# Two prompt tiles served head by head: an interleaved job order and a shorter lead-in

## The chip, the core and the metric

The kernel runs on one NeuronCore of a Trainium2 chip. The metric is the device time of one execution in microseconds. The engines are TensorE (PE), VectorE (DVE), ScalarE (ACT), GpSimd (POOL, which here issues the gathers) and SyncE (SP, which issues plain loads). Each executes its own instructions in program order and waits on semaphores. All loads run on the core's 16 DMA engines.

## What is computed

One step of a hybrid decoder layer for a prompt of 512 tokens and a sample group of 32, in float32. The trunk (S5 scan, convolution module, cross-attention, three gates and `w_out`) gives `h`; then comes the part that takes most of the time, a layer of 16384 single-neuron experts:

```python
q = (xb @ w_q).reshape(tb, 8, 2, 128)                 # 8 heads, two halves
s = einsum('thpc,pkc->thpk', q, sub_keys)             # 128 scores for each half
sv, si = top_k(s, 16)
cand = sv[:, :, 0, :, None] + sv[:, :, 1, None, :]    # 16 x 16 sums
cv, ci = top_k(cand.reshape(tb, 8, 256), 16)          # 16 experts per token and head
gate = softmax(cv)
act = gelu(einsum('thkd,td->thk', u_tab[experts], xb))
out = einsum('thk,thkd->td', gate * act, v_tab[experts])
```

and at last `y = rmsnorm(h + out)`.

## The kernel before

**Tiles and jobs.** Tokens lie in tiles of 128: t = 0 to 3 for the prompt, t = 4 for the samples, which share two jobs. A job is a pair (t, h) of tile and head; there are 34 in the list `EXPERTS`, and each gathers 16 times: gather g = 16·n + j fetches, for job n and choice j, one row of u and v (8 KB together) for each of 128 tokens, 1.05 MB in all.

**Trunk first for the first 256 tokens.** The trunk runs for tokens 0 to 255 (tiles 0 and 1) before the experts begin. Head 0's queries are made beside the last products of `w_out`. `first_query`/`first_queries` make the queries of one head for both tiles (jobs `Aq{h}.{b}` on the PSUM banks, 8 matmuls each), `first_scores` the scores (`As{h}.{b}`, two matmuls each), again for both tiles at once. ACT copies them to the score buffers `sc(n)`, one per job. `EARLY_HEADS` heads have queries and scores made ahead of the expert loop (with the query of one more head).

**The late list.** Everything else on PE, in `rest_of_trunk`, is threaded through the loop: the other heads of tiles 0 and 1, then for tokens 256 to 543 the gates and projections (`g{q}.{b}` with 8 matmuls, `p{q}.{b}` with 4), `w_out` (`w0` to `w7`), 15 empty steps, the sum of squares (`ssb`), transposes (`ht`, `xt`), queries `q{h}.{b}` (8 each) and scores `s{h}.{b}` (3 each). One step of this list, a matmul or an empty step, is called a unit here. After each gather j PE does 2 units, or 6 where j % 4 is 3 (`late_matmuls`). `PLACE[name]` is the gather in whose units a job ends. DVE and ACT do their part of a late job at a fixed number of gathers behind PLACE: DVE multiplies and adds a gate product at PLACE + 8 (L1926, L1931), adds a `w` job at PLACE + 8 (L1937), and ACT copies `ht` jobs at PLACE + 2 (L1344). Before `w0` PE waits until the last merge is done (`pe.wait_ge(mergeb_ok, 2 * KD)`). DVE reads `ssb` at PLACE + 8 (L1940) and two gathers later makes the 8 blocks of `xbT_b` (L1943 to L1949).

**The loop on each engine.**
- DVE: for each gather a dot product with u (`dot`, L1876); every fourth, behind j % 4 = 0, `weigh` (L1891) makes the weights of the four gathers before; for the jobs 0 to 11 the choices 3, 7, 11, 15 are added by DVE itself (`add_row`, L1902, behind the dot with j % 4 = 1); behind j = 10 `add_rest` (L1915) adds PE's sum of the job before to `h2(t)`. Between the dots it executes pieces of `route(n + 2)`, the two top-16 searches that give job n + 2 its experts. `route(0)` and `route(1)` run ahead of the loop.
- ACT: per four gathers a gelu (L1274), per PE gather a scaled identity matrix (`diag`, L1407), once a job the exponentials of the softmax (`exp_of`, L1267).
- PE: for each gather not added by DVE, two matmuls of 512 columns with the scaled identity (L1058), and then the units.
- POOL issues gather g into a ring of `RING = 10` rows when row g − 10 has been used: `pool.wait_ge(v_used[by], count)`.
- SP loads weight tiles of 512 KB (projections 256 KB) into four places, the m-th when the product of the (m − 4)-th is done.

In the trace one float32 matmul counts as two entries.

## Time and profile before

| | us |
|---|---|
| median of 3 runs | 1969.55 (1967.14 to 1969.92) |
| the profiled execution | 1968.79 |
| its span on the core | 1967.2 |
| first gather issued at | 469.35 |
| busy in the span: PE / DVE / POOL / ACT | 1697.1 / 1367.2 / 661.6 / 526.7 |
| moved by the DMA engines | 674.10 MB, of which gathers (software queue) 577.23 MB |
| first entries of the chain that ended last, by engine | PE 47%, DMA 36%, issue 8% |

Times in the rows are in us from the start of the span. In the order of time a row gives its start, its length, engine, line, operation, output and input, how many entries it joins, and in brackets how long the engine was idle before and who released it. In a table of stretches a row gives the stretch, its length, the busy time of PE, PEld, DVE, ACT and POOL with the number of instructions, then the granted clock of PE (1.00 is the level of 2.4 GHz, 0.50 that of 1.2), the busy share of the DMA engines and what they moved in GB/s.

### The profile page before, as it was taken

The page shows a single profiled execution, that of the slowest core. Times are in us where ns is not written, and L with a number is a line of the kernel's source. Part 1 is how long each engine was busy: PE and PEld are TensorE (multiplying, and loading weights), DVE is VectorE, ACT ScalarE, POOL GpSimd, SP SyncE. Part 2 cuts the span into 40 slices and gives each one's busy share as a digit, 9 for nine tenths or more (in the row PEclk, how much of TensorE's full clock was granted, in tenths as well). Part 3 has the DMA queues.
Part 4 walks back from the last instruction along what each step waited for, and adds up shares of the span by engine and source line. Part 5 has one row for each costly group of instructions (what it writes and reads, how often), then busy time and mean ns, then how long its engine had stood idle before and what let it go on. Part 6 is the DMA issues. An engine that isn't in the chain of part 4 may idle for free.

```text
span 1967.2 us, 17805 instructions
## 1 busy us (share of the span) xinstructions
PE 1697.1 (86%) x5491; PEld 1011.1 (51%) x5491; DVE 1367.2 (69%) x3363; ACT 526.7 (27%) x1211; POOL 661.6 (34%) x605
## 2 busy tenths in 40 slices
PE   8999999999899999978989987778777767767876
PEld 7888887888555555544455543333333212323332
DVE  5998573334777777767977667777777777777755
ACT  3121143202243433312333322222222212222221
POOL 1020030001344444433443444434434444444442
PEclk9989999999999999989899999988989999998899
DMA  5452453555999999989999999999999999999996
GB/s 208 138 86 97 159 126 118 154 181 206 419 419 418 418 417 416 416 329 420 385 422 419 407 389 421 421 421 417 413 417 415 421 421 417 414 422 396 414 421 286
DMA packets 112111, 674.10 MB, mean 343 GB/s; under 512 B 12720, under 2 KB 15104, under 8 KB 42000
## 3 DMA queue, kind: packets, MB, share of 16 engines
q0 software_dynamic: 80816, 577.23, 72.2%
q1 hardware_dynamic: 30640, 94.82, 14.0%
q10 hardware_dynamic: 560, 0.92, 0.2%
q8 instruction: 44, 0.72, 0.1%
q14 instruction: 51, 0.42, 0.1%
HBM read 665.79 MB, written 6.21 MB: 342 GB/s over the span
## 4 chain that ended last, share of the span: by engine, by line
PE 47%; DMA 36%; issue 8%; DVE 4%; ACT 2%; POOL 2%; ACTq 0%; POOLq 0%; DVEq 0%; SPq 0%
DMA upper<-in_peer_uv,upper 22%; PE pair L1058 19%; DMA lower<-in_peer_uv,upper 13%; PE pair L616 7%; PE pair L627 6%; PE pair L979 5%; PE pair L929 2%; PE pair L810 1%; ACT upper L1407 1%; DVE upper L1876 1%; POOL upper L592 1%; POOL lower L592 1%; PE pair L661 1%; PE pair L671 1%; PE pair L798 1%
## 5 line engine op out<-in xcount | busy, mean ns | idle before, releaser
L1058 PE MATMUL pair<-upper 128*128 128x512 f32 (+1 forms) x1184 | 582.7, 635 | 135.8 <-ACT upper L1407 135.8
L592 POOL DMA_INDIRECT upper<-in_peer_uv,upper x324 | 372.8, 1151 | 493.4 <-PE pair L1058 429.6
L1058 PE MATMUL pair<-lower,upper 128*128 128x512 f32 (+1 forms) x792 | 383.9, 627 | 92.8 <-ACT upper L1407 92.8
L1058 PEld LDWEIGHTS pair<-upper 128*128 128x128 f32 (+1 forms) x1184 | 225.9, 197 | 430.0 <-issue 281.6
L592 POOL DMA_INDIRECT lower<-in_peer_uv,upper x220 | 249.3, 1133 | 498.7 <-PE pair L1058 316.0
L1058 PEld LDWEIGHTS pair<-lower,upper 128*128 128x128 f32 (+1 forms) x792 | 149.8, 195 | 286.9 <-issue 188.5
L1876 DVE CUSTOM_DVE_ANT_0 upper<-upper 128x1024 f32<-128x1024 f32 x172 | 210.7, 1225 | 121.5 <-DMA upper<-in_peer_uv,upper 121.5
L1876 DVE CUSTOM_DVE_ANT_0 upper<-upper,lower 128x1024 f32<-128x1024 f32 x152 | 186.0, 1224 | 97.4 <-DMA upper<-in_peer_uv,upper 97.2
L1407 ACT ACTIVATE upper<-upper 128x128 f32<-128x128 f32 (+1 forms) x494 | 164.7, 386 | 296.2 <-DVE upper L1891 296.0
L1876 DVE CUSTOM_DVE_ANT_0 lower<-lower,upper 128x1024 f32<-128x1024 f32 x116 | 142.1, 1225 | 87.8 <-DMA lower<-in_peer_uv,upper 87.7
L1274 ACT ACTIVATE upper<-upper 128x4 f32<-128x4 f32 x136 | 33.7, 248 | 627.3 <-DVE upper L1876 627.2
L979 PE MATMUL pair<-lower 128*128 128x288 f32 x704 | 185.1, 407 | 0.0
L1876 DVE CUSTOM_DVE_ANT_0 lower<-lower 128x1024 f32<-128x1024 f32 x104 | 127.2, 1223 | 71.1 <-DMA lower<-in_peer_uv,upper 71.0
L979 PEld LDWEIGHTS pair<-lower 128*128 128x128 f32 x704 | 133.7, 191 | 65.9 <-issue 37.7
L616 PE MATMUL pair<-lower 128*128 128x272 f32 x576 | 133.1, 393 | 1.5 <-ACT lower L1138 1.5
L616 PEld LDWEIGHTS pair<-lower 128*128 128x128 f32 x576 | 109.3, 190 | 24.5 <-issue 2.2
L979 PE MATMUL pair<-upper,lower 128*128 128x288 f32 x256 | 72.2, 416 | 10.7 <-DVE upper L1931 10.7
L1603 DVE SCALAR_TENSOR_TENSOR upper<-upper 128x512 f32<-128x512 f32 x120 | 80.5, 745 | 0.0
L627 PE MATMUL pair<-lower 128*128 128x256 f32 x336 | 75.4, 379 | 0.0
L979 PEld LDWEIGHTS pair<-upper,lower 128*128 128x128 f32 x256 | 49.9, 196 | 43.2 <-issue 22.5
L1274 ACT ACT_TABLE_LOAD x56 | 71.8, 1283 | 1.0
L627 PEld LDWEIGHTS pair<-lower 128*128 128x128 f32 x336 | 63.3, 190 | 8.4
(364 smaller groups left out, 1736.3 us busy)
## 6 DMA issues: line engine op xcount, KB each, us to landing
lower<-in_w_in SPq DMA_DIRECT2D x64, 512.0 KB, 7.2
lower<-in_peer_q SPq DMA_DIRECT2D x32, 512.0 KB, 8.0
lower<-in_proj SPq DMA_DIRECT2D x48, 256.0 KB, 7.0
lower<-in_w_out SPq DMA_DIRECT2D x16, 512.0 KB, 4.6
upper<-in_peer_uv,upper POOLq DMA_INDIRECT x324, 11.7
upper<-in_cache_k SPq DMA_DIRECT2D x8, 512.0 KB, 4.5
upper<-in_cache_v SPq DMA_DIRECT2D x8, 512.0 KB, 3.7
lower<-in_peer_uv,upper POOLq DMA_INDIRECT x220, 11.7
```

The costliest lines, as they stand in the source:

```text
L592: pool.indirect_dma_start(row(g), None, a["peer_uv"], bass.IndirectOffsetOnAxis(ap=idx[:, n % 8, j:j + 1], axis=0)).then_inc(row_in[g % RI ...
L616: mm = pe.matmul(ps[:, h, 0:HT], w[:, j, :], rhs[:, j, h * HT:(h + 1) * HT], start=(j == 0), stop=(j == k - 1))
L627: mm = pe.matmul(one_bank(ps), w[:, j, :], rhs[:, j, 0:FIRST], start=(j == 0), stop=(j == k - 1))
L661: mm = pe.matmul(ps[:, 0, 0:MEM], w[:, k, :], memT[:, k, :], start=(k == 0), stop=(k == KD - 1))
L671: mm = pe.matmul(ps[:, m, (j - 1) * P:(j + 1) * P], memT[:, k, m * P:(m + 1) * P], wring[:, s0:s0 + 2, k * P:(k + 1) * P], start=(k == 0), ...
L929: mm = pe.matmul(ps[:, 0:FIRST], w[:, k, :], xbT[:, k, :], start=(k == 0), stop=(k == KD - 1))
L979: mm = pe.matmul(ps[:, 0:REST], w[:, j, :], x[:, j, :], start=(j == 0), stop=(j == k - 1))
L1058: mm = pe.matmul(pairs[n % 2][0:rows, h, :], diag[:, (nth - 1) % DIAGS, 0:rows], row(g)[:, D + h * 512:D + (h + 1) * 512], start=(j == min ...
L1274: act.activation(gel[:, n % 2, j:j + GROUP], dots[:, n % 2, j:j + GROUP], ACT.Gelu, scale=rcol[:, t:t + 1] if t < 2 else 1.0).then_inc(gel ...
L1407: act.activation(diag[:, nth % DIAGS, 0:cols], turn, ACT.Copy, scale=weight[:, n % 8, j:j + 1]).then_inc(diag_ok, 1)
L1603: stt(v, tail, w, v, ALU.mult, ALU.add).then_inc(conv_step, 1)
L1876: dve.tensor_tensor_reduce(u, u, xb(EXPERTS[n][0]), 1.0, 0.0, ALU.mult, ALU.add, dots[:, n % 2, j:j + 1]).then_inc(u_used, 1)
```

## The change

Three edits. The list of jobs: the sixteen jobs of the tiles 0 and 1 alternate between the tiles, (0,0), (1,0), (0,1), (1,1) and so on, where they were (0,0) to (0,7) and then (1,0) to (1,7); the jobs from 16 on stay. `EARLY_HEADS` goes from 4 to 2. And ACT writes the scores of head h to the buffers 2h and 2h + 1, with the two exponentials `exp_of(0)` and `exp_of(1)` both behind the scores of head 1.

```diff
-EARLY_HEADS = 4
+EARLY_HEADS = 2
...
-EXPERTS = ([(t, h) for t in range(3) for h in range(PH)] + [(4, 0), (4, 1)] + [(3, h) for h in range(PH)])
+EXPERTS = ([(t, h) for h in range(PH) for t in range(2)] + [(2, h) for h in range(PH)] + [(4, 0), (4, 1)] + [(3, h) for h in range(PH)])
...
-                    act.activation(sc(h)[:, b, :], ps[:, 0:P], ACT.Copy, scale=rcol[:, 0:1])
-                    act.activation(sc(8 + h)[:, b, :], ps[:, P:2 * P], ACT.Copy, scale=rcol[:, 1:2]
+                    act.activation(sc(2 * h)[:, b, :], ps[:, 0:P], ACT.Copy, scale=rcol[:, 0:1])
+                    act.activation(sc(2 * h + 1)[:, b, :], ps[:, P:2 * P], ACT.Copy, scale=rcol[:, 1:2]
...
-                if h != 2:
-                    exp_of(h // 2)
+            for n in range(LAG):
+                exp_of(n)
```

`BANK_JOBS` and `PLACE` are worked out from `EARLY_HEADS`. The jobs Aq3, As2, Aq4 and As3 enter the late list with 16, 4, 16 and 4 units. PLACE moves so:

| job | before | after |
|---|---|---|
| As2.1 | ahead of the loop | 7 |
| As7.1 | 21 | 35 |
| p7.2 | 117 | 131 |
| w0 | 119 | 133 |
| ssb | 147 | 159 |
| q7.1 | 217 | 231 |
| s7.1 | 226 | 239 |

On PE, ahead of the loop and at its first gather (L929 are queries, L944 scores, L1058 the gather's product), one piece of the difference:

```order
 L929 MATMUL pair<-upper,lower 128x256 x32
 L944 MATMUL pair<-upper,lower 128x128 x4
-L929 MATMUL pair<-upper,lower 128x256 x16
-L944 MATMUL pair<-upper,lower 128x128 x4
-L929 MATMUL pair<-upper,lower 128x256 x16
-L944 MATMUL pair<-upper,lower 128x128 x4
 L1058 MATMUL pair<-lower,upper 128x512 x2
```

The queries of heads 3 and 4 and the scores of heads 2 and 3 are no longer there.

On PE, at the entry to w0 (the L979 that waits for `mergeb_ok`), before: behind gather 118, with 8 matmuls up to gather 120.

```order
L1058 MATMUL pair1<-upper 128x512 [waits diag_ok]
L1058 MATMUL pair1<-upper 128x512
L979 MATMUL pair3<-upper,lower 128x288 [waits bank_free2,late_w_in0,mergeb_ok]
L979 MATMUL pair3<-upper,lower 128x288 x7
L1058 MATMUL pair1<-lower,upper 128x512 [waits diag_ok]
```

After: behind gather 130 and the last four matmuls of p7.2, with 4 matmuls up to gather 132.

```order
L1058 MATMUL pair0<-lower,upper 128x512
L979 MATMUL pair2<-upper,lower 128x288 [waits bank_free1,late_w_in3]
L979 MATMUL pair2<-upper,lower 128x288 x3
L979 MATMUL pair3<-upper,lower 128x288 [waits bank_free2,late_w_in0,mergeb_ok]
L979 MATMUL pair3<-upper,lower 128x288 x3
L1058 MATMUL pair0<-lower,upper 128x512 [waits diag_ok]
```

The place moved by 12 gathers on PE, and w0 is cut in other pieces (4, 2 and 2 matmuls where 8 stood in a row).

On DVE, at that last merge (L1931), before: behind the dot of gather 125, which is one behind a weighing.

```order
L1876 ISA upper<-upper,lower 128x1024 [waits row_in5]
L1876 ISA upper 128x1
L1902 SCALAR_TENSOR_TENSOR upper<-lower,upper 128x1024 [waits acc_step,w_ok]
L1926 TENSOR_TENSOR lower<-lower,pair2 128x288 [waits acc_step,bank_full1,bank_free0]
L1931 TENSOR_TENSOR upper<-upper,lower 128x288 [waits bank_free1,mergeb_ok]
```

After: behind the dot of gather 139, with L1915 just ahead of that dot.

```order
L1915 TENSOR_TENSOR upper<-upper,pair1 128x1024 [waits v_used_by_pe,acc_step]
L1876 ISA upper<-upper,lower 128x1024 [waits row_in9]
L1876 ISA upper 128x1
L1860 TENSOR_TENSOR upper<-upper 128x256 [waits dve_step]
L1863 TENSOR_REDUCE upper<-upper 128x16 [waits dve_step]
L1926 TENSOR_TENSOR lower<-lower,pair2 128x288 [waits bank_full1,bank_free0]
L1931 TENSOR_TENSOR upper<-upper,lower 128x288 [waits bank_free1,mergeb_ok]
```

The merge moved by 14 gathers on DVE, w0's first matmul by 12 on PE.

## Rows read from the trace of the kernel before

**Rows 1.** The page, the DMA rate in 40 equal slices of the span

```profile
GB/s 208 138 86 97 159 126 118 154 181 206 419 419 418 418 417 416 416 329 420 385 422 419 407 389 421 421 421 417 413 417 415 421 421 417 414 422 396 414 421 286
```

**Rows 2.** Table of stretches, columns as told above

```profile
470.00:838.00 368.00, 340.12 (x1153) 213.12 (x1152) 275.44 (x691) 135.48 (x254) 159.42 (x125) 1.00 1.01 416
860.00:870.00 10.00, 10.00 (x29) 6.40 (x28) 5.91 (x13) 1.62 (x5) 1.59 (x1) 0.82 0.23 72
...
940.00:980.00 40.00, 35.16 (x112) 19.36 (x111) 37.25 (x88) 12.33 (x30) 19.30 (x15) 0.91 0.96 376
980.00:1110.00 130.00, 121.52 (x404) 71.46 (x404) 93.47 (x232) 39.13 (x117) 51.12 (x46) 0.96 1.02 420
1110.00:1150.00 40.00, 40.00 (x137) 23.96 (x136) 25.97 (x68) 13.67 (x42) 15.55 (x14) 1.00 0.97 364
```

**Rows 3.** Order of time at the loop's start, end of route(0) and gathers 0 and 10

```profile
468.89 0.17 DVE L1869 CAST upper<-upper 128x16 uint32<-128x16 f32 x1
...
469.35 1.01 POOL L592 DMA_INDIRECT lower<-in_peer_uv,upper  x1 [141.12 <-DVE upper L1869]
...
499.36 0.94 POOL L592 DMA_INDIRECT lower<-in_peer_uv,upper  x1 [17.78 <-PE pair L1058]
```

**Rows 4.** Order of time there, DVE, ACT and PE

```profile
478.51 0.49 DVE L1808 MAX8 upper<-lower 128x8 f32<-128x128 f32 x2 [9.44 <-ACT lower L1298]
...
487.82 1.22 DVE L1876 CUSTOM_DVE_ANT_0 lower<-lower 128x1024 f32<-128x1024 f32 x1
...
478.43 1.28 ACT L1267 ACT_TABLE_LOAD   x1
...
477.51 7.07 PE L929 MATMUL pair<-upper,lower 128*128 128x256 f32 x32
...
496.59 1.95 PE L1058 MATMUL pair<-lower,upper 128*128 128x512 f32 x4 [3.32 <-ACT upper L1407]
```

**Rows 5.** Order of time around the entry to w0, DVE, PE and POOL

```profile
840.55 0.16 DVE L1891 TENSOR_TENSOR upper<-upper 128x4 f32<-128x4 f32 x1
...
849.35 1.21 DVE L1915 TENSOR_TENSOR upper<-upper,pair 128x1024 f32<-128x1024 f32 x1
...
858.76 0.46 DVE L1931 TENSOR_TENSOR upper<-upper,lower 128x288 f32<-128x288 f32 x1
...
860.58 1.23 DVE L1876 CUSTOM_DVE_ANT_0 upper<-upper,lower 128x1024 f32<-128x1024 f32 x1 [0.21 <-DMA upper<-in_peer_uv,upper]
...
846.67 1.88 PE L1058 MATMUL pair<-upper 128*128 128x512 f32 x4
859.28 6.31 PE L979 MATMUL pair<-upper,lower 128*128 128x288 f32 x16 [10.73 <-DVE upper L1931]
...
850.59 1.92 POOL L592 DMA_INDIRECT upper<-in_peer_uv,upper  x1 [0.30 <-issue]
868.11 1.59 POOL L592 DMA_INDIRECT lower<-in_peer_uv,upper  x1 [15.60 <-PE pair L1058]
```

**Rows 6.** Table of stretches, two more around the first gap

```profile
860.00:862.00 2.00, 2.00 (x6) 1.43 (x5) 1.60 (x4) 0.00 (x0) 0.00 (x0) 0.50 0.15 61
...
870.00:880.00 10.00, 10.00 (x35) 6.35 (x35) 4.04 (x16) 0.00 (x0) 4.49 (x4) 1.00 0.95 342
```

**Rows 7.** Order of time in the second gap, PE and DVE

```profile
956.92 0.39 PE L989 MATMUL pair<-upper 128*32 128x128 f32 x1 [3.23 <-ACT lower L1344]
...
957.29 1.95 DVE L1943 RECIPROCAL upper<-upper 128x288 f32<-128x288 f32 x1
...
964.01 0.26 DVE L1949 COPY lower<-lower 128x192 f32<-128x192 f32 x1
```

**Rows 8.** Order of time ahead of the third gap, PE (gathers 200, 216) and SP

```profile
1091.57 1.88 PE L1058 MATMUL pair<-lower,upper 128*128 128x512 f32 x4
...
1139.17 1.88 PE L1058 MATMUL pair<-upper 128*128 128x512 f32 x4
...
1010.19 92.16 SPq L496 DMA_DIRECT2D lower<-in_peer_q  x10
```

## The prediction

> **What bounds the kernel now.** I read the slices of the page first, then stretches of DMA rate, then the order of time on single engines. The DMA rate stands at 413 to 423 GB/s in most slices from the eleventh on [rows 1]; the first gather is issued at 469.35, and 470 to 838 runs at 416 GB/s and a DMA share of 1.01 [rows 2, 3]. So from the first gather on the 16 DMA engines set the end: end = first gather + bytes / rate + the times in which the engines had nothing to move. The bytes are 544 gathers of 1.05 MB (2.49 us each at 421 GB/s) and the weight tiles of 512 KB (1.25 us). PE is busy for 340 of those 368 us [rows 2], yet it does not set the end there.
>
> The lost times before the ring's tail are three, priced as (1 − rate/420) × length. Gap 1, around 860: 8.3 us in 860 to 870 and 1.9 in 870 to 880, with the first edge at 858 some 10.5 us [rows 2, 6]. Gap 2, 940 to 980: 40 × (1 − 376/420) = 4.2 us. Gap 3, 1110 to 1150: 5.3 us [rows 2]. The change has to be weighed by what it does to these three and to the first gather.
>
> **Part 1, the start: 0.** Route(0) ends on DVE at 469.06 and releases the first gather at 469.35 [rows 3]; PE and ACT do the same up to there in both kernels, so this time stays. What does come earlier is the first dot product. Route(1) now takes the scores of head 0 that are there already, instead of waiting until 478.51 for head 1 [rows 4]. It takes 8.9 us, so it ends at about 478.0; the exponential of job 0, whose table ACT loads at 478.43, and the normalising on DVE put the first dot near 480.4 instead of 487.82, 7.4 us earlier. PE drops the queries of heads 3 and 4 in front of the loop (32 matmuls, which the trace counts as 64 entries, 7.07 us for each head as at 477.51) and 8 short score matmuls [rows 4]. The first gather's product then waits for four landed gathers and not for PE: gathers 0 to 3 and four weight tiles are 6.3 MB, landed near 487, so the product moves from 496.59 to about 492, and gather 10 from 499.36 to about 494.5. But the DMA engines had no idle time between the first and the eleventh gather: eight weight tiles and ten gathers filled it, and four of these tiles (those of heads 5 and 6) now come after it. The same bytes are moved in another order. Ten gathers and four tiles last until about 500, so gather 10 is still in time. Bounds: −7.4 us if the earlier dots passed through to the end, +0 to +3 if the engines ran dry before gather 10; I take 0, the row nearest to it being 470 to 838 at share 1.01 [rows 2].
>
> All that is left out ahead of the loop is done in it: 40 matmuls of the late list (32 queries, 8 scores), three per gather on average, so everything behind them moves back by 13 to 14 gathers. Their PE time (about 17 us) lies in the DMA-bound stretch, where PE had 28 us free of 368. If that cover were gone they would cost these 17 us.
>
> **Part 2, gap 1: +2.2.** Here PE enters w0, the first tile of w_out, and waits for DVE's last merge (P7.2), which DVE does only 8 gathers after P7.2's place. The L1915 at 849.35 follows dot 122, so the weighing at 840.55 follows dot 120, and the merge at 858.76 follows dot 125 [rows 5]. PE has done gather 118 (846.67), vector row 119 is freed by DVE, so gathers up to 129 may be issued (the last at 850.59); PE stands from 848.4 to 859.28; eight matmuls of w0 take 6.31 us; then comes gather 120, which frees a slot at 868.11 [rows 5]. Since 860 to 862 shows 61 GB/s [rows 6], the engines ran dry at about 859.5.
> After the change w0 starts behind gather 130 and vector row 131, again the last ones of a group of four, so again nine gathers beyond the weighing may be issued and the dry point stays. But the merge is due at dot 139, seven after the weighing at dot 132, not five. That dot corresponds to the one at 860.58; with its own 1.15 us, the accumulator addition L1915 that now falls on dot 138 (about 0.8 of it not hidden) and the two merge steps (0.95), PE restarts at 863.5 by before's clock, 4.2 us later. Only four matmuls of w0, not eight, stand before the next gather's product: at 6.31/8 = 0.79 each that would give 3.2 us back, and since the first ones after a stand run at the lower clock level I count 0.97 for each that stays and get 2.4. Net +1.8, less 0.2 for the weight tiles that reach into the window; the tile that filled 1.2 us of the gap before (it waits for the whole of w0) now comes behind it, of which I count half, +0.6. Sum +2.2, bounds 0 and +6.2 (two gathers, 5.0, and the tile, 1.2, with nothing given back).
> The Trainium skill (DMA: Bandwidth & Descriptors, Where 436 GB/s comes from) says that for loads from HBM a core is held to about 358 GB/s. The trace shows 416 over 368 us [rows 2], so it is not so here. By 358 a gather would be an estimated 2.93 us and the upper bound of this part 0.9 us higher; the sum stands on 421.
>
> **Part 3, gap 2: −0.5.** PE waits 3.23 us for ACT's copy of ht2.0, until 956.92, and only behind that starts gather 152; DVE spends 957.29 to 964.27 on xbT_b [rows 7]. In the new order the matmul that needs that copy stands behind gather 164 (which is what 152 was), and PE starts it about 2.4 us earlier. The wait behind it stays: no weighing before DVE is through with xbT_b, and L1915 now stands between that and the next weighing (+1.2). So earlier slots are followed by a later one. Bounds −2.4 and +1.2; I take −0.5.
>
> **Part 4, gap 3: +1.7.** From job 12 on (gather 192) DVE adds no rows, and PE carries all 16 beside the late list. There 16 gathers take 1091.57 to 1139.17, 2.975 us each [rows 8]; DMA needs 2.49, and while weight tiles still come (two per 22 units, 7.33 gathers) 2.83. The last tile is issued by 1102.35 [rows 8], and the loss begins behind it, since 980 to 1110 is full at 420 [rows 2]. Before, the late list ends at gather 226; now at 239. The 16 or so gathers behind the last tile stay as they are; 13 more gathers run with tiles at 2.975 against 2.83, 13 × 0.145 = 1.9 us. Bounds 0 (slack takes it) and +3; I take +1.7.
>
> **Sum.** 1968.79 (profiled execution, span 1967.2) + 0 + 2.2 − 0.5 + 1.7 = 1972.2. The median before is 0.76 above the profiled execution; I put the forecast between the two readings, at **1972.5**.
>
> **Rivals.**
> (a) *The head start passes through*, faster. Mechanism: the 7.4 us at the first dot shift every later slot. It decides if the DMA rate dips between 480 and 507 in the kernel before. Against it: share 1.01 in 470 to 838 and no dip. Time 1968.8 − 7.4 + 0, about 1961.4. The Trainium skill (Perfetto Trace Analysis, Optimization Strategy) advises to make the dependencies of the engine's gaps start sooner; by it this would be the result. The rows show that engine's gaps elsewhere, at 860, 940 and 1110.
> (b) *Gap 1 grows by both gathers in full*, slower. Place: PE between the two matmuls of P7.2 and w0. It decides if gather 141 is read before DVE reaches dot 139 and the matmuls before the restart don't get shorter. 1968.8 + 6.2 − 0.5 + 1.9 = 1976.4.
> (c) *The regrouping at gap 2 wins and gap 3 has slack*: +1.1 − 2.4 + 0, about 1967.5.
> (d) *The change does not do what it says*: scores of head 2 late for route(4), so that DVE blocks. As2 is done at gather 7 and needed at 32; for it speaks nothing. 1970 to 1975.
>
> **How the numbers follow.** Forecast 0.50, (a) 0.08, (b) 0.28, (c) 0.12, (d) 0.02. A measurement can tell 0.2%, 3.9 us: same is 1965.6 to 1973.5. The forecast's own range is 1969 to 1975.5; a fifth of its chance, 0.10, lies above 1973.5, and 0.04 of (c) lies below 1965.6; the rest of (c) and (d) are within. Faster 0.12, same 0.50, slower 0.38. The range 1965 to 1978 takes in the forecast, (c) and most of (b) and leaves out (a) and the upper tail, under 2 in 10.
>
> **What would show it.** Right: first gather near 469.4, first dot near 480, first L1058 near 492, DMA at 416 with no dip until gap 1; the gap lies 13 gathers (about 40 us) later and is 12 to 13 us long; the full-PE stretch before gap 3 is some 39 us longer. Wrong: any idle DMA between 480 and 850; a gap 1 of over 15 or under 10 us; gap 2 gone.

## The result, and the profile after

| | before | after |
|---|---|---|
| median, us | 1968.39 (1963.88 to 1971.73, 11 runs) | 1975.45 (1973.17 to 1977.7, 11 runs) |
| the profiled execution, and its span | 1968.79, 1967.2 | 1976.74, 1975.1 |
| ratio to before | | 1.0037, 95% interval 1.0027 to 1.0046 |

The change makes the kernel 7.1 us slower, 0.37%. The time lies inside the predicted range (1965 to 1978), 3 us above the predicted 1972.5, and on the "slower" side of the 0.2% line where the likeliest class was "same". The two profiled executions differ by 7.9 us in their spans, so they show the same thing as the medians.

PE and DVE are busy for as long as before (1700.5 and 1366.7 us), POOL 10 us less (651.8). The page's DMA rate in 40 slices, of the changed kernel, answers to [rows 1]:

```profile
GB/s 209 136 86 96 156 128 117 159 175 219 419 419 415 418 418 413 419 418 291 421 362 418 419 385 408 422 421 422 421 418 422 404 422 409 412 421 417 414 422 278
```

The dip of gap 1 has gone one slice back (from the 18th, 329, to the 19th, 291) and is deeper; that of gap 2 from the 20th (385) to the 21st (362); gap 3 keeps its 385 to 389 in the 24th.

**The start.** POOL, DVE, PE and POOL again in order of time, and one stretch, of the changed kernel. They answer to [rows 3, 4]:

```profile
469.54 1.00 POOL L592 DMA_INDIRECT lower<-in_peer_uv,upper  x1 [141.12 <-DVE upper L1869]
...
480.69 1.22 DVE L1876 CUSTOM_DVE_ANT_0 lower<-lower 128x1024 f32<-128x1024 f32 x1
...
491.32 3.40 PE L1058 MATMUL pair<-lower,upper 128*128 128x512 f32 x4 [13.45 <-ACT upper L1407]
...
495.54 1.78 POOL L592 DMA_INDIRECT lower<-in_peer_uv,upper  x1 [12.82 <-PE pair L1058]
...
480.00:490.00 10.00, 0.00 (x0) 0.00 (x0) 7.46 (x23) 2.00 (x6) 2.41 (x2) 0.53 1.02 426
```

The first gather starts when it did (469.54 against 469.35), the first dot is 7.1 us earlier (480.69 against 487.82), and gather 10 is issued 3.8 us earlier (495.54 against 499.36). PE stands 13.45 us for nothing but landed rows, its granted clock at 0.53 from 480 to 490, near the 1.2 GHz level, and the DMA engines are full meanwhile (share 1.02).

**The three gaps.** Stretches of the changed kernel; columns as in [rows 2]. The ones of 10 us answer to [rows 2, 6], the long ones are the measure by which the runs below are compared, with those of the kernel before in the second fence:

```profile
890.00:900.00 10.00, 4.64 (x9) 3.20 (x10) 9.31 (x21) 0.99 (x3) 0.00 (x0) 0.50 0.08 32
900.00:910.00 10.00, 10.00 (x33) 6.11 (x32) 1.69 (x3) 0.74 (x2) 3.86 (x3) 0.98 0.58 224
910.00:920.00 10.00, 10.00 (x34) 6.08 (x33) 3.35 (x9) 1.62 (x5) 3.75 (x4) 1.00 0.97 375
...
888.00:890.00 2.00, 0.00 (x0) 0.00 (x0) 1.82 (x4) 0.00 (x0) 0.00 (x0) 0.50 0.94 393
890.00:892.00 2.00, 0.00 (x0) 0.00 (x0) 1.97 (x5) 0.00 (x0) 0.00 (x0) 0.50 0.27 111
...
1060.00:1150.00 90.00, 90.00 (x309) 54.00 (x308) 59.70 (x157) 27.99 (x90) 35.07 (x32) 1.00 1.02 420
...
840.00:940.00 100.00, 81.23 (x256) 49.61 (x255) 66.57 (x161) 24.25 (x49) 34.16 (x29) 0.91 0.87 355
940.00:1060.00 120.00, 99.11 (x295) 53.80 (x294) 95.57 (x228) 33.54 (x79) 47.98 (x41) 0.89 0.96 396
1060.00:1220.00 160.00, 156.01 (x515) 90.42 (x514) 107.60 (x289) 51.54 (x160) 67.03 (x59) 1.00 1.00 405
```

```profile
840.00:940.00 100.00, 81.81 (x238) 47.54 (x237) 70.76 (x172) 21.78 (x50) 33.00 (x30) 0.90 0.93 376
940.00:1060.00 120.00, 107.26 (x348) 61.45 (x347) 98.41 (x231) 35.90 (x97) 50.04 (x44) 0.93 1.00 406
1060.00:1220.00 160.00, 145.61 (x433) 77.27 (x432) 110.79 (x297) 48.02 (x142) 64.80 (x61) 0.98 1.00 407
```

By (1 − rate/420) × length, gap 1 is 9.2 + 4.7 + 1.1 = 15.0 us (10.5 before). By the long stretches, 840 to 940 loses 15.5 us (10.5), 940 to 1060 loses 6.9 (4.0), and 1060 to 1220 loses 5.7 (5.0). Together 8.6 us more, of a span that is 7.9 longer. So nearly the whole loss lies in gaps 1 and 2 (5.0 and 2.9 us). Each of these numbers is from one execution, and the rates are whole GB/s, so a stretch of 100 us carries an error of some 0.1 to 0.3 us.

**Gap 1**, in order of time on DVE, PE and POOL of the changed kernel; it answers to [rows 5]:

```profile
869.09 0.16 DVE L1891 TENSOR_TENSOR upper<-upper 128x4 f32<-128x4 f32 x1
...
885.99 1.23 DVE L1876 CUSTOM_DVE_ANT_0 upper<-upper,lower 128x1024 f32<-128x1024 f32 x1 [1.95 <-DMA upper<-in_peer_uv,upper]
...
894.84 0.46 DVE L1931 TENSOR_TENSOR upper<-upper,lower 128x288 f32<-128x288 f32 x1
...
877.00 2.10 PE L979 MATMUL pair<-upper,lower 128*128 128x288 f32 x8
895.36 4.21 PE L979 MATMUL pair<-upper,lower 128*128 128x288 f32 x8 [16.26 <-DVE upper L1931]
899.36 2.42 PE L1058 MATMUL pair<-lower,upper 128*128 128x512 f32 x4
...
879.21 1.58 POOL L592 DMA_INDIRECT lower<-in_peer_uv,upper  x1 [0.30 <-issue]
902.59 0.94 POOL L592 DMA_INDIRECT lower<-in_peer_uv,upper  x1 [21.79 <-PE pair L1058]
```

PE waits for the last merge with the gathers' own products queued behind that wait. It stands for 16.26 us where it stood for 10.73, and POOL waits 21.79 us for a free row where it waited 15.60 [rows 5]. The four matmuls of w0 behind the stand take 4.21 us, four of the same kind ahead of it 2.10: they run at the lower clock level.

**Gap 2**, DVE, PE and POOL of the changed kernel; the second fence is DVE in the kernel before, the two weighings on either side of the block in [rows 7]:

```profile
987.75 0.16 DVE L1891 TENSOR_TENSOR upper<-upper 128x4 f32<-128x4 f32 x1
...
992.19 1.94 DVE L1943 RECIPROCAL upper<-upper 128x288 f32<-128x288 f32 x1
...
999.26 0.26 DVE L1949 COPY lower<-lower 128x192 f32<-128x192 f32 x1
...
1001.37 1.21 DVE L1915 TENSOR_TENSOR upper<-upper,pair 128x1024 f32<-128x1024 f32 x1
...
1005.58 0.16 DVE L1891 TENSOR_TENSOR upper<-upper 128x4 f32<-128x4 f32 x1
...
999.57 1.33 PE L979 MATMUL pair<-lower 128*128 128x288 f32 x2 [2.87 <-DVE lower L1949]
1006.22 3.67 PE L1058 MATMUL pair<-upper 128*128 128x512 f32 x4 [5.32 <-ACT upper L1407]
...
1010.71 1.36 POOL L592 DMA_INDIRECT upper<-in_peer_uv,upper  x1 [11.53 <-PE pair L1058]
```

```profile
954.03 0.16 DVE L1891 TENSOR_TENSOR upper<-upper 128x4 f32<-128x4 f32 x1
...
967.62 0.15 DVE L1891 TENSOR_TENSOR upper<-upper 128x4 f32<-128x4 f32 x1
```

Between two weighings lie four dots and, once, the block `xbT_b`. That interval was 13.59 us and is 17.83: the block takes 7.2 us (6.9 before), but in the changed kernel L1915 (1.1 us net) and pieces of route share it (2.4 us, and 0.4 more right behind the first weighing). No product of a gather can be made before the weighing. PE waits twice there: 2.87 us for the end of the block (the queries q0.0 read it), and then 5.32 us more for the identity matrix that ACT scales by the weights. The second of these waits ends last, and behind it POOL has waited 11.53 us for a free row.

### The profile page after: what moved, and what is told of

Same layout as the page of the kernel before. It is cut to its first block, busy times and chain, and to the rows that moved or that the text cites. A ratio compares the mean times of both kernels' runs of the same rounds, so it can differ in the third digit from the quotient of the medians.

```text
span 1975.1 us, 17805 instructions
## 1 busy us (share of the span) xinstructions
PE 1700.5 (86%) x5491; PEld 1012.6 (51%) x5491; DVE 1366.7 (69%) x3363; ACT 526.2 (27%) x1211; POOL 651.8 (33%) x605
## 4 chain that ended last, share of the span: by engine, by line
PE 42%; DMA 34%; issue 15%; DVE 4%; POOL 3%; ACT 2%; ACTq 0%; POOLq 0%; DVEq 0%; SPq 0%
PE pair L1058 20%; DMA upper<-in_peer_uv,upper 19%; DMA lower<-in_peer_uv,upper 14%; PE pair L979 7%; PE pair L616 6%; POOL upper L592 2%; PE pair L810 1%; PE pair L627 1%; ACT upper L1407 1%; POOL lower L592 1%; DVE upper L1876 1%; PE pair L661 1%; PE pair L671 1%; PE pair L798 1%; DVE lower L1876 1%
## 5 line engine op out<-in xcount | busy, mean ns | idle before, releaser
L1058 PE MATMUL pair<-upper 128*128 128x512 f32 (+1 forms) x1184 | 581.8, 634 | 131.9 <-ACT upper L1407 131.6
L592 POOL DMA_INDIRECT upper<-in_peer_uv,upper x324 | 366.7, 1132 | 503.5 <-PE pair L1058 437.8
L1058 PE MATMUL pair<-lower,upper 128*128 128x512 f32 (+1 forms) x792 | 390.6, 635 | 96.9 <-ACT upper L1407 96.8
L1058 PEld LDWEIGHTS pair<-upper 128*128 128x128 f32 (+1 forms) x1184 | 225.2, 196 | 425.2 <-issue 275.8
L1058 PEld LDWEIGHTS pair<-lower,upper 128*128 128x128 f32 (+1 forms) x792 | 151.9, 198 | 290.2 <-issue 198.2
L979 PE MATMUL pair<-lower 128*128 128x288 f32 x704 | 192.0, 409 | 2.9 <-DVE lower L1949 2.9
L979 PEld LDWEIGHTS pair<-lower 128*128 128x128 f32 x704 | 134.2, 192 | 77.0 <-issue 47.7
L979 PE MATMUL pair<-upper,lower 128*128 128x288 f32 x256 | 69.4, 415 | 16.3 <-DVE upper L1931 16.3
L979 PEld LDWEIGHTS pair<-upper,lower 128*128 128x128 f32 x256 | 49.6, 194 | 42.2 <-DVE upper L1931 16.7
```

Of the source, the lines that this page charges most:

```text
L592: pool.indirect_dma_start(row(g), None, a["peer_uv"], bass.IndirectOffsetOnAxis(ap=idx[:, n % 8, j:j + 1], axis=0)).then_inc(row_in[g % RI ...
L979: mm = pe.matmul(ps[:, 0:REST], w[:, j, :], x[:, j, :], start=(j == 0), stop=(j == k - 1))
L1058: mm = pe.matmul(pairs[n % 2][0:rows, h, :], diag[:, (nth - 1) % DIAGS, 0:rows], row(g)[:, D + h * 512:D + (h + 1) * 512], start=(j == min ...
```

## The experiments

Every run below was set against its own runs of the kernel before (medians 1967.78 for the first four, 1968.26 for the next four, 1968.69 for the last four). "Over after" is the difference of the distances to these medians. The stretches are of one profiled execution each, and that can lie off its median: by 4.5 us below it in the run with 36 units and 3.5 us below in the early merge of the changed kernel, by 2.9 us above with the 23 empty units and 3.1 above with the block in four in the kernel before. Part of this is the time ahead of the loop: the first gather is issued between 466.60 and 469.84 us in the fourteen traces.

**Is it the order of the jobs, or the shorter lead-in?** The changed kernel with four heads made early again:

```diff
-EARLY_HEADS = 2
+EARLY_HEADS = 4
...
                 first_score(h)
-            for n in range(LAG):
-                exp_of(n)
+                if h == 1:
+                    for n in range(LAG):
+                        exp_of(n)
```

> The changed kernel with four heads made ahead of the loop again: only the order of the jobs is changed against the kernel before, and both first exponentials stand behind the scores of head 1. The late list lies where it lay (w0 at gather 119, last score at 226). Theory P (the 7 us come from where the late list's waits fall in the loop): the loop's three gaps are those of before, 10.5, 4.2 and 5.3 us, and the time is before's within 2 us, 1966.5 to 1970.5. Rival O (the head-by-head order itself costs, by the alternation of the two accumulators or the other score buffers): 1973 to 1976, as in the changed kernel.

Measured 1967.26 us, ratio 1.0000 (0.9991 to 1.0009). Its 840 to 940 and 940 to 1060 lose 10.0 and 4.0 us, as in the kernel before. The order head by head costs and gives nothing; the loss comes with the shorter lead-in.

**Is it the later late list alone?** The kernel before, whose lead-in is whole, with 40 empty units ahead of `g0.0`:

```diff
+BANK_JOBS += [("gapL", 40)]
 for _q in range(KD):
...
                 yield from first_heads(EARLY_HEADS, PH)
+                for _ in range(40):
+                    yield
```

> The kernel before (tile by tile, four heads ahead) with 40 empty steps put into the late list ahead of the first late gate, so that everything from there on lies at the gathers of the changed kernel (w0 at 133, last score at 239). No work is added. Theory P: all of the change's loss comes back, gap 1 at 14 to 15.5 us, gap 2 at 6.5 to 7.5, gap 3 at 5.3 to 6; 1974 to 1977. Rival W (the loss is the work of two heads that now runs in the loop): an empty step costs nothing, 1967 to 1970.

Measured 1976.98 us, ratio 1.0046 (1.0033 to 1.006). Its stretches and its stand at w0:

```profile
840.00:940.00 100.00, 81.40 (x257) 49.66 (x256) 67.27 (x163) 24.69 (x49) 33.43 (x29) 0.91 0.88 358
940.00:1060.00 120.00, 96.89 (x289) 52.96 (x288) 94.00 (x221) 32.38 (x75) 46.93 (x42) 0.89 0.96 392
...
895.71 4.21 PE L980 MATMUL pair<-upper,lower 128*128 128x288 f32 x8 [16.25 <-DVE upper L1934]
```

14.8 and 8.0 us are lost, and PE stands for 16.25 us. Nothing of the computation has moved here but the places of the late list, so the whole loss, and a little more, comes from these places. That matmuls moved into the loop costs nothing by itself; the next run, which has them in the loop, shows the same.

**Does lateness cost, or the place within the period?** The changed kernel with 8 more empty units, a shift of 48 units in all: 16 gathers, one whole job (12 units per four gathers).

```diff
+BANK_JOBS += [("gapL", 8)]
...
+                for _ in range(8):
+                    yield
```

> The changed kernel with 8 empty steps ahead of the first late gate: the late list then lies 48 units, exactly one job (16 gathers), behind before's, so that each wait falls on the same choice number j as before (w0 at 135, sum of squares at 163). Theory P: gap 1 goes back to 10 to 11 us, gap 2 to 4 to 5, gap 3 stays at 5.3 to 7.5; 1968 to 1971.5, though the early part is that of the changed kernel, whose first dot comes 7 us sooner. Rival W: as the changed kernel, 1974 to 1977. If the head start were worth its 7 us: 1961 to 1964.

Measured 1968.63 us, ratio 1.0006 (0.9997 to 1.0016). Later by 8 units, and faster by 6.2 us. Stretches, and the stand at w0:

```profile
840.00:940.00 100.00, 88.83 (x277) 54.30 (x276) 69.51 (x171) 28.49 (x55) 36.84 (x31) 0.93 0.94 381
940.00:1060.00 120.00, 100.46 (x310) 55.92 (x309) 99.11 (x238) 34.24 (x86) 51.65 (x43) 0.93 1.00 409
...
896.82 6.49 PE L980 MATMUL pair<-upper,lower 128*128 128x288 f32 x16 [7.79 <-DVE upper L1934]
```

9.3 and 3.1 us, as before or less. Every wait is in the place of its job that it had before, and the loss is gone. It is also the cleanest reading of the head start: this kernel has its first dot at 479.18, 11.2 us behind its first gather (468.02), where the kernel before needs 18.5 us, and its time is that of the kernel before. The head start is worth nothing.

**Which period?** The kernel before with 36 empty units: 12 gathers, three whole groups of four but not a whole job. It puts w0 in the same place of its group (behind gather 130, before 118) and ssb where the changed kernel has it.

> The kernel before with 36 empty units ahead of g0.0 (three whole rounds of 12 units) instead of the 40 of the earlier run. w0 then starts behind gather 130, in the same place of its group of four as before (118), while ssb ends at 159 as in the changed kernel. Theory P (the loss is the place of PE's and DVE's waits against the periodic work, and gap 1 hangs on the place in the group of four, gap 2 on what DVE has beside the block in the job): gap 1 stays at 9.5 to 11.5 us as before, gap 2 becomes 6.5 to 7.5 us as in the changed kernel; time 2 to 4 us over the kernel before, ratio 1.001 to 1.002. Rival R (what counts in gap 1 too is the place within the job of 16, where route and L1915 fall): gap 1 becomes 13 to 15 us and the time that of the changed kernel, +7 to +9 us. Rival S (every later late list costs, by its length): 36/40 of the loss, +6 to +8 us, spread over both gaps.

```profile
840.00:940.00 100.00, 85.11 (x273) 52.12 (x272) 69.01 (x171) 25.51 (x52) 33.77 (x31) 0.95 0.92 370
940.00:1060.00 120.00, 97.87 (x300) 53.75 (x299) 96.86 (x227) 31.79 (x81) 53.31 (x42) 0.93 0.97 395
```

The stretches came out near what was expected: 11.9 us (expected 9.5 to 11.5 for gap 1; PE stands for 12.02) and 7.1 us (6.5 to 7.5). So gap 1 goes mostly by the place in the group of four and gap 2 by the place in the job. The time did not: 1974.6 us, ratio 1.0033 (1.0022 to 1.0045), over the expected 1.001 to 1.002. It is 6.3 us over its own runs of the kernel before, which is what rival S gave (36/40 of the loss). Against rival S, that lateness by itself costs, stand the 11.9 us of gap 1, where it gives over 14, and the 48 units, which lie later and cost nothing. The profiled execution, 1970.06, is the fastest of its six runs, so the trace shows the run that lost least; where four of the other five lose 4.4 to 5.2 us more isn't seen.

**Gap 1's cause.** The changed kernel with the last merge 4 gathers earlier, behind dot 135:

```diff
-                        yield PLACE[f"p{q}.{b}"] + 8
+                        yield PLACE[f"p{q}.{b}"] + (4 if (q, b) == (KD - 1, 2) else 8)
```

> The changed kernel with DVE's last merge (of P7.2) due 4 gathers behind its place instead of 8, at dot 135 instead of 139; all else stays. Theory P: PE restarts with w0 near 882 instead of 895.4, the ring does not run dry, gap 1 falls from 15 us to 0 to 3; 1960 to 1965. Rival S (DVE is so loaded there that the engines wait for it anyway, the stand of PE being only its sign): gap 1 of over 8 us, 1968 or more.

Measured 1966.16 us, ratio 0.9991 (0.9982 to 1.0), 8.7 us under the changed kernel and 1.2 over the expected 1960 to 1965:

```profile
840.00:940.00 100.00, 90.09 (x286) 54.11 (x285) 73.89 (x179) 26.17 (x54) 39.43 (x32) 0.98 1.00 410
940.00:1060.00 120.00, 98.75 (x309) 55.12 (x308) 95.08 (x233) 35.20 (x90) 48.90 (x43) 0.91 0.95 388
...
930.00:940.00 10.00, 7.46 (x17) 4.00 (x18) 8.68 (x18) 2.81 (x6) 1.66 (x2) 0.83 0.87 341
940.00:950.00 10.00, 10.00 (x31) 5.71 (x30) 7.51 (x18) 2.06 (x6) 5.71 (x5) 1.00 0.98 378
...
880.11 2.21 PE L979 MATMUL pair<-upper,lower 128*128 128x288 f32 x8 [3.33 <-DVE upper L1931]
```

The stand is 3.33 us and the stretch loses 2.4 us instead of 15.5. Gap 1 is that one wait: no stretch of 10 us between 850 and 930 moves under 411 GB/s now. 13.1 us are gained there, 2.2 given back in 940 to 1060. Both the 2.4 us that are left and the 2.2 lie mostly in new, small dips from 930 to 950 and from 960 to 980 (378 and 397 GB/s), where the changed kernel moved 409 to 425; the first of them stands behind an interval of 15.74 us between two weighings (916.15 and 931.89). Gap 2 itself is as long as it was: 990 to 1010 loses 7.0 us, and in the changed kernel 1000 to 1020 does. Why the first dip comes only when gap 1 is gone was not tested.

The same with the merge 6 gathers behind its place (dot 137), to see whether the gap follows the merge or jumps:

> The changed kernel with the last merge due at PLACE + 6, behind dot 137, instead of +8 (dot 139) or +4 (dot 135, whose run lost 3.4 us in 840 to 950 against 15.5). Theory P: the gap follows the time at which the merge is done, one for one: dots 138 and 139 with L1915 took 6.4 us (889.37 and 892.43, the merges at 882.2 and 894.84 as the two ends), so 840 to 950 loses 8 to 10 us, and gap 2 as in the changed kernel 6.5 to 8.5; time 4 to 7 us below the changed kernel, 1968.5 to 1971.5. Rival T (a threshold: either the next group of four is in time or not): as with +4 (3 to 4 us, time near 1966) or as with +8 (15 us, near 1975).

840 to 940 loses 9.5 us at a stand of 11.08: between the two ends, close to one for one, and no threshold. But the time, 1972.83 us (1.0020, 1.0011 to 1.0029), is only 2.9 us under the changed kernel where 4 to 7 were expected: 940 to 1060 loses 8.3 us instead of 6.9.

**The clock in gap 1.** 26 more matmuls of w0's weights fill PE's stand, their sums overwritten by the real ones:

```diff
+                w, ps = late_weights("w0"), begin_bank("w0")
+                for _ in range(26):
+                    pe.matmul(ps[:, 0:REST], w[:, 0, :], nT[:, 0, FIRST:], start=True, stop=True)
                 pe.wait_ge(mergeb_ok, 2 * KD)
...
```

> The changed kernel with 26 more matmuls of 128x128 by 288 (of w0's weights, their sums overwritten by the real ones) on PE between the last matmul before the wait for the merges and that wait. At 0.525 us each (8 took 4.2 us at full clock) they fill 13.6 of the 16.3 us in which PE stands in gap 1. Theory C (part of the gap is the lower clock behind the stand: w0's four matmuls took 4.21 against 2.10 and the next product 2.42 against 1.88): the granted clock stays near 1.00 through 895, the restart stays at its time and POOL's next issue comes 2 to 2.7 us earlier; gap 1 12.3 to 13 us, time 2 to 3 us below the changed kernel. Rival: the clock falls all the same or the matmuls push the restart later: no gain or up to +1 us.

```profile
878.21 12.77 PE L1004 MATMUL pair<-lower 128*128 128x288 f32 x52
894.26 3.89 PE L1007 MATMUL pair<-upper,lower 128*128 128x288 f32 x8 [3.28 <-DVE upper L1939]
...
894.00:896.00 2.00, 1.74 (x4) 1.31 (x5) 1.93 (x9) 0.54 (x2) 0.00 (x0) 0.57 0.02 8
```

Measured 1975.55 us, ratio 1.0038 (1.0026 to 1.0051): no gain. The granted clock stood at 1.00 through the filler, and yet behind the 3.28 us without work it was 0.57 (894 to 896), so w0's matmuls took 3.89 us instead of 4.21. 840 to 940 loses 12.6 us instead of 15.5; the part of it that the clock can have given is 0.3 + 0.5 (the next product 1.88 instead of 2.42), and the restart itself came 1.1 us earlier. 940 to 1060 loses 8.6 instead of 6.9. So this run doesn't settle what the clock costs in this gap, nor whether the time hangs on it: the filler kept the clock up only until PE stood again, and w0 ran at the lower level all the same.

**Gap 2's cause.** The changed kernel with 23 instead of 15 empty units ahead of ssb, so that the block comes behind dot 173 (j = 13), its place in the job before (dot 157 there):

```diff
-BANK_JOBS += [(f"w{_j}", KD) for _j in range(KD)] + [("gap0", 15), ("ssb", KD)]
+BANK_JOBS += [(f"w{_j}", KD) for _j in range(KD)] + [("gap0", 23), ("ssb", KD)]
...
-                for _ in range(15):
+                for _ in range(23):
                     yield
                 ps = begin_bank("ssb")
```

> The changed kernel with 23 instead of 15 empty units ahead of ssb: ssb ends at gather 163 (j = 3) instead of 159 (j = 15), so the block xbT_b comes before dot 173 (j = 13), the place in its job that it had before. Theory P: gap 1 stays at 14 to 16 us; gap 2 goes from 6.9 to 4 to 4.7 us; time 2 to 3 us below the changed kernel, 1972 to 1974, ratio to the kernel before 1.002 to 1.003. Rival (gap 2 is long because gap 1 left the engines in another state): gap 2 stays at 6.5 to 7.5 and the time at 1975 to 1977.

```profile
940.00:1060.00 120.00, 98.58 (x294) 53.41 (x293) 100.97 (x240) 33.48 (x78) 49.22 (x44) 0.90 1.00 410
```

2.9 us instead of 6.9, gap 1 as in the changed kernel (14.3), time 1971.65 us (1.0017, 1.0008 to 1.0025), 3.7 us under the changed kernel. The interval between the weighings is 13.87 us instead of 17.83. The expectation held, the gain somewhat larger, and the rival falls: gap 1 stayed and gap 2 shrank.

Then the block cut in four, a quarter behind each of four dots:

```diff
...
                                     ).then_inc(xbTb_ok, 2)
+                    if k < KD - 1:
+                        yield PLACE["ssb"] + 10 + (k + 1) // 2
...
+                for _ in range(8):
+                    yield
                 pe.wait_ge(xbTb_ok, KD)
```

> The changed kernel with the block xbT_b on DVE cut in four: two of its eight products (and their copy) behind each of four dots in a row instead of all eight behind one, and 8 more empty units ahead of q0.0 so that PE does not stand waiting for the last quarter. Theory B (gap 2 is the time in which no weighing is made because DVE is 7.3 us in the block, plus what lies between it and the next weighing): with about 1.9 us of it between two dots the rows are weighed on time, gap 2 goes from 6.8 to 0 to 3 us, time 4 to 7 us below the changed kernel, 1968.5 to 1971.5. Rival Q (gap 2 comes from PE's wait for the copy of ht2.0 or from q0.0): gap 2 stays at 5 us or more.

```profile
940.00:1060.00 120.00, 96.73 (x284) 51.52 (x283) 98.67 (x234) 31.88 (x77) 49.85 (x42) 0.90 0.97 397
...
985.06 0.16 DVE L1893 TENSOR_TENSOR upper<-upper 128x4 f32<-128x4 f32 x1
...
1001.81 0.16 DVE L1893 TENSOR_TENSOR upper<-upper 128x4 f32<-128x4 f32 x1
...
1002.46 5.90 PE L1060 MATMUL pair<-upper 128*128 128x512 f32 x8 [8.43 <-ACT upper L1409]
```

6.6 us: gap 2 stayed, and the time, 1973.4 us (1.0022, 1.0013 to 1.0031), missed the expected 1968.5 to 1971.5. My form of the theory was wrong: the block's being in one piece doesn't matter. Three of the quarters fall in the same group of four dots, so the interval between its two weighings is 16.75 us, 1.08 less than 17.83, the one quarter that now lies behind the second weighing. What counts is all that DVE has to do between two weighings. That gap 2 stayed at over 5 us is also what rival Q gave, and the 23 empty units had moved its two waits as well, so the times alone don't part the two; the traces do. In this run PE waits neither for the copy of ht2.0 nor for the block: it is through with its work at 994.0 and then stands 8.43 us for the identity matrix behind the weighing (L1409). In the changed kernel there is no wait for the copy either, and the one for the block ends 6.7 us before the one for the weighing. In the kernels with a short interval the copy does hold PE (3.23 us before, 2.77 with 23 units), so what is left of gap 2 there, 3 to 4 us, need not come from the interval; that was not tested.

**Versions that beat both kernels.** The early merge in the kernel before; the same with the block in four; and the changed kernel with the early merge and the 23 empty units.

> The kernel before, with the last merge (P7.2) due 4 gathers behind its PLACE instead of 8: behind dot 121 instead of dot 125. The same edit took 9 us from the changed kernel. Theory P: gap 1 (10.5 us) goes down to 0 to 2, gap 2 stays at 4 to 6 and gap 3 at 5 to 6; span 1956 to 1960, time 7 to 11 us below the kernel before, ratio 0.9945 to 0.9965. Rival: what is late next (gap 2, since the DMA engines are ahead and the ring is fuller or emptier there) takes back half or more: ratio 0.998 to 0.999.

1962.15 us, ratio 0.9972 (0.9961 to 0.9983). That is 6.1 us under its own runs of the kernel before, less than the 7 to 11 expected: PE doesn't stand at w0 at all any more, but 840 to 940 still loses 4.5 us, 2.7 of them from 920 to 940, and 940 to 1060 loses 4.9.

> The kernel before with both edits: the last merge due at PLACE + 4 and the block xbT_b cut in four with 8 more empty units ahead of q0.0. From the merge alone the median was 1962.15. If both gaps hang on these two waits: 840 to 1060 loses 2 to 6 us instead of 9.4, span 1957 to 1961, time 1957 to 1961, ratio 0.994 to 0.9965. If the loss in 920 to 950 that stood behind the gap that was taken away has another cause: 1961 to 1963.

1961.78 us, ratio 0.9963 (0.9949 to 0.9976); the four quarters add nothing that can be told from 1962.15. 840 to 1060 loses 9.0 us where 2 to 6 were expected, so the two gaps don't hang on these two waits alone.

> The changed kernel with the last merge due at PLACE + 4 and 23 instead of 15 empty units ahead of ssb. Each alone: 840 to 950 lost 3.4 us (against 15.5), and 950 to 1060 lost 2.9 us (against 6.8). If the two add: 840 to 1060 loses 6 to 8 us, gap 3 4.5 to 5.5; span 1956 to 1960, time 1960 to 1964, ratio 0.996 to 0.998. If gap 2 grows once gap 1 is gone (it was 8.4 with the merge alone): 950 to 1060 loses 5 or more and the time is 1964 to 1967.

1961.97 us, ratio 0.9963 (0.995 to 0.9977), as expected. 840 to 940 loses 3.6 us, 940 to 1060 5.1, 1060 to 1220 5.0; the first two together, 8.7, are a little over the expected 6 to 8. It is 13.8 us under the measured changed kernel, of which the two edits alone gave 8.7 and 3.7, and about as fast as the kernel before with the early merge: with both waits in a good place there is again nothing between the two lead-ins.

**All runs.** Stand: PE's idle time at the entry to w0. Interval: between the two weighings around the block. Losses in us by (1 − rate/420) × length.

| kernel | us | ratio | stand | 840 to 940 | interval | 940 to 1060 |
|---|---|---|---|---|---|---|
| before | 1968.39 | | 10.73 | 10.5 | 13.59 | 4.0 |
| order only | 1967.26 | 1.0000 | 10.72 | 10.0 | 13.58 | 4.0 |
| before, shift 36 | 1974.6 | 1.0033 | 12.02 | 11.9 | 17.76 | 7.1 |
| before, shift 40 | 1976.98 | 1.0046 | 16.25 | 14.8 | 17.83 | 8.0 |
| before, early merge | 1962.15 | 0.9972 | 0 | 4.5 | 13.59 | 4.9 |
| before, early merge, block in four | 1961.78 | 0.9963 | 0 | 3.6 | 12.36 | 5.4 |
| after | 1975.45 | 1.0037 | 16.26 | 15.5 | 17.83 | 6.9 |
| after, shift 48 in all | 1968.63 | 1.0006 | 7.79 | 9.3 | 13.68 | 3.1 |
| after, merge + 6 | 1972.83 | 1.0020 | 11.08 | 9.5 | 17.85 | 8.3 |
| after, merge + 4 | 1966.16 | 0.9991 | 3.33 | 2.4 | 18.04 | 9.1 |
| after, filler | 1975.55 | 1.0038 | 3.28 | 12.6 | 17.78 | 8.6 |
| after, 23 empty units | 1971.65 | 1.0017 | 16.22 | 14.3 | 13.87 | 2.9 |
| after, block in four | 1973.4 | 1.0022 | 16.26 | 15.0 | 16.75 | 6.6 |
| after, merge + 4, 23 units | 1961.97 | 0.9963 | 3.46 | 3.6 | 14.12 | 5.1 |

The loss of the first stretch goes with the stand (but for the filler, where the stand is filled and the wait is the same); with stands of 0 to 3.5 us there remain 2.4 to 4.6, which lie elsewhere in the stretch. The loss of the other goes with the interval: 12.4 to 14.1 us go with 2.9 to 5.4, 16.8 to 18.0 with 6.6 to 9.1. These are two groups; within the first the longer interval doesn't lose more. As an account of the whole: each profiled span, less the time of its first gather and the losses of the three stretches, leaves 1477 to 1481 us in all fourteen traces, while the spans themselves run from 1958.8 to 1977.9. So there is no large fourth place in which these kernels differ.

## Why the prediction was right where it was right, and too low by 3 us

**What bounds the kernel, and Part 1 (0).** Right. The end was taken as first gather plus bytes plus the times without DMA work, and the loss appeared in these times alone. The first gather, the first dot (480.69 for "near 480.4"), the first L1058 (491.32 for "about 492") and gather 10 (495.54 for "about 494.5") came as worked out, and nothing of the 7 us passed through: rival (a) falls, and the run with 48 units shows it a second time. The Trainium skill (Perfetto Trace Analysis, Optimization Strategy) would have the dependencies of the engine's gaps start sooner. For this head start the trace gives nothing to it, since the DMA engines had no gap there (share 1.02); for the merge, which is the dependency of a real gap, it agrees: 8.7 us.

**Part 2, gap 1 (+2.2, measured +4.5 to +5.0).** The mechanism and its place were right: dot 139, seven behind the weighing, four matmuls before the next product. The size was off in three terms.
- The restart was put 4.2 us later by before's clock. From the weighing to the restart it took 859.28 − 840.55 = 18.7 us before [rows 5] and 895.36 − 869.09 = 26.3 after, 7.5 us more. I let dots 133 to 139 run in the time that the dots 121 to 127 took, but they took 24.5 us from the dot at 867.94, against 21.2. Of these 3.3 us, 2.6 are DVE's waits for landed rows (1.95 before the dot at 885.99 and four more, 5.9 in sum, against 3.3 from 843.17 to 860.58). DVE isn't slower there, it goes at the pace of the DMA engines.
- That same pace moved the dry point: the engines ran dry at about 889.9 (888 to 890 still moved 393 GB/s, 890 to 892 only 111), 10.7 us behind POOL's last issue, where it had been 8.9 (859.5 against 850.59 [rows 5, 6]). That gives back some 1.8 us where I had 0.2.
- The shorter matmuls gave back 1.6 us (from the restart to POOL's issue, 8.83 to 7.23), not 2.4; they ran at 1.05 us each, not 0.97, and the next product was slow too (2.42).

7.5 − 1.8 − 1.6 = 4.1, and with the tile that no longer fills the gap near the 4.5 of the 10-us stretches. It lay inside the bounds of 0 to 6.2.

**Part 3, gap 2 (−0.5, measured +2.7 to +2.9).** The step that failed. PE started gather 164 earlier, as foreseen (0.6 us behind the weighing instead of 3.1), but that was no gain: POOL's rows up to there were issued well before the engines needed them. And of what follows the block only L1915 (+1.2) was counted. The term should have been the whole interval between the two weighings, 13.59 against 17.83 us: on both sides of the block lay pieces of route as well (2.4 us), which at j = 13 to 15 are through and at j = 9 to 12 are not. This is outside the bounds of −2.4 to +1.2 that I gave.

**Part 4, gap 3 (+1.7, measured +0.7).** 1060 to 1220 loses 5.7 us instead of 5.0. The 13 gathers more with PE full did not cost 0.145 us each; 1060 to 1150 ran at 420 GB/s with PE busy throughout, so the ring's slack took most of it, the lower bound's reason.

**The sum and the chances.** +2.2 − 0.5 + 1.7 = +3.4 was expected and about +8 came in the trace, +7.1 in the medians. Rival (b) came closest with 1976.4, by a gap 1 of +6.2 that was too large and a gap 2 that was too small: the time was near, the parts were not. The chance of "slower", 0.38, was too low for a sum whose own terms were mostly positive and whose largest was bounded by 6.2 above and 0 below.

That the measured time lies in the range, and just inside the end of the forecast's own 1969 to 1975.5, is in part luck: two of the three terms were too low, one of them with the wrong sign, and the third, too high by 1.0, took some of it back.

**Its own signs.** Of what would show it right, the start came as said and no dip came before gap 1. But gap 1 came 12 gathers and 30 us later (the engines dry at 889.9 instead of 859.5), as Part 2 has it, and not 13 and about 40. Its length, 15.0 us by the short stretches and 15.5 by the long one, is not the 12 to 13 that were to show the prediction right; it stands at the 15 above which it was to be wrong. The loss of gap 3 begins at 1160 instead of 1110.

**What stays open.** Where gap 1 was shortened in the changed kernel, 940 to 1060 lost 1.4 to 2.2 us more than without it. For the merge at +4 that is the new dips and not gap 2; for the merge at +6 and the filler it is gap 2 itself (8.2 and 8.5 us instead of 7.0). But the kernel before with 40 units loses 8.0 there with a gap 1 of 14.8. How gap 2 hangs on gap 1, and where four of the other five runs of the 36 units lose their time, isn't settled.

## What to carry to other kernels

If the DMA engines are full from the first transfer on, as they were here, an earlier start of the engines behind them is worth nothing; look only at the stretches in which they run dry, and at the one wait behind which the freeing of the buffers is queued. A list of extra work threaded through a periodic loop has a phase: shift it by whole periods, or work out anew for each in-order wait what else its engine does in that part of the period (here 40 units cost 7 to 9 us, 48 cost nothing). And cost such a wait by the interval between the two events that release buffers, not by the length of the block that stands in it.

## What the chip showed that was not expected

The granted clock after a short stand differs between two kernels that look alike there. In the changed kernel with the early merge PE stood for 3.33 us, and w0's four matmuls took 2.21 us, the time at the 2.4 GHz level. With the filler PE had been busy for 12.77 us at 1.00, stood for 3.28 us, and the same four matmuls took 3.89, at a granted clock of 0.57. With the early merge and 23 empty units a stand of 3.46 us was followed by 3.90 us (0.65 in the first 2 us), although PE had done the same work ahead of it as with the early merge alone, and the granted clock had been 1.00 in both. So a stand of 3.3 to 3.5 us doesn't by its length tell at which of the two levels PE starts again.
